# Routing one token tile ahead of the other, expert totals by 256 columns per bank, and one wave of last scatters

## The reference, cut to what matters

```
for l in range(DEPTH):                                   # 2 layers
    x = x + mixer(rms_norm(x)) @ w_out[l]
    h = rms_norm(x, norm_ffn_g[l])                       # 256 tokens
    g_idx = argmax(h @ wg + bg)                          # one group of 4
    top_val, top_idx = top_k(((h @ we + be) in group g_idx), 2)   # two of its 8 experts
    gates = softmax(groups)[g_idx] * softmax(top_val)
    y_e = (silu(h_e @ w_gate[e]) * (h_e @ w_up[e])) @ w_down[e]   # per expert e, its tokens h_e
    x = x + sum over the two experts of gates * y_e
```

## Time and profile before

| what | value |
|---|---|
| median of 3 runs | 1178.26 us (1177.89 to 1180.73) |
| profiled execution | 1179.48 us, span 1176.5 us |
| TensorE matmul busy | 884.6 us (75%) |
| VectorE busy | 469.5 us (40%) |
| ScalarE busy | 172.6 us (15%) |
| moved by DMA | 442.23 MB, mean 376 GB/s |
| TensorE clock granted, mean | 0.908 |

### The profile page before, as it was taken

How to read it: one execution, slowest core, us unless ns; L and a number is a source line. 1 busy time by engine, 2 the same in 40 slices (tenths; PEclk the granted TensorE clock), 3 DMA queues, 4 the chain that set the end, 5 groups by cost and what they waited for, 6 DMA issues and landing times.

```text
span 1176.5 us, 20445 instructions
## 1 busy us (share of the span) xinstructions
PE 884.6 (75%) x8557; PEld 531.7 (45%) x8557; DVE 469.5 (40%) x1263; ACT 172.6 (15%) x483; POOL 43.3 (4%) x98
## 2 busy tenths in 40 slices
PE   9999998675657565647799999977565666666777
PEld 6577574342424242424465675744233332323343
DVE  2967474331323232313239674743232322322222
ACT  2334211110000000100113442110000000000001
POOL 2001120000000000000000120000000000000000
PEclk9999998897979897988899999999889887879789
DMA  8946589999999999999996275999999999999996
GB/s 278 387 181 248 226 330 428 426 427 428 428 428 429 428 428 429 429 428 425 411 387 272 73 278 187 380 428 427 428 426 428 429 428 428 428 428 429 428 425 273
DMA packets 56141, 442.23 MB, mean 376 GB/s; under 512 B 9472, under 2 KB 12560, under 8 KB 30992
## 3 DMA queue, kind: packets, MB, share of 16 engines
q1 hardware_dynamic: 56080, 441.37, 90.8%
HBM read 440.30 MB, written 1.05 MB: 375 GB/s over the span
## 4 chain that ended last, share of the span: by engine, by line
PE 47%; DMA 44%; DVE 5%; issue 2%; SPq 1%; ACT 0%; DVEq 0%; POOL 0%; POOLq 0%
DMA ring<-in_expert_w_up 40%; PE psum L884 13%; PE psum L917 8%; PE psum L926 6%; PE psum L1001 5%; DMA work<-in_expert_w_down 4%; PE psum L898 3%; PE psum L763 3%; PE psum L857 2%; PE psum L1018 1%; PE psum L949 1%; DVE work L1522 1%; SPq L475 1%; PE psum L1128 1%; PE psum L744 1%
## 5 line engine op out<-in xcount | busy, mean ns | idle before, releaser
L884 PE MATMUL psum<-ring,work 128*32 128x256 f32 x3712 | 262.6, 444 | 111.3 <-DMA ring<-in_expert_w_up 111.3
L884 PEld LDWEIGHTS psum<-ring,work 128*32 128x32 f32 x3712 | 147.4, 127 | 224.3 <-issue 178.5
L898 PE MATMUL psum<-ring,work 128*32 128x256 f32 x1664 | 125.8, 454 | 126.6 <-DVE work L1528 126.2
L1520 DVE TENSOR_SCALAR work<-work 128x128 f32<-128x128 f32 x62 | 14.2, 229 | 344.0 <-ACT work L1206 344.0
L898 PEld LDWEIGHTS psum<-ring,work 128*32 128x32 f32 x1664 | 56.9, 128 | 191.5 <-DVE work L1528 148.8
L1533 DVE COPY work<-psum 32x256 f32<-32x256 f32 x124 | 52.6, 424 | 136.0 <-PE psum L898 134.9
L917 PE MATMUL psum<-ring,hT 128*128 128x512 f32 x224 | 98.5, 594 | 1.7 <-ACT work L1229 1.7
L1210 ACT ACTIVATE work<-psum 32x256 f32<-32x256 f32 x124 | 46.2, 373 | 267.1 <-PE psum L898 266.4
L763 PE MATMUL psum<-work,h 128*128 128x128 f32 x512 | 65.5, 290 | 14.2 <-issue 12.9
L763 PEld LDWEIGHTS psum<-work,h 128*128 128x128 f32 x512 | 64.3, 205 | 23.5 <-issue 23.5
L1206 ACT ACTIVATE work<-psum 128x128 f32<-128x128 f32 x62 | 17.2, 277 | 369.0 <-PE psum L884 339.7
(11 more groups left out here) (299 smaller groups left out, 780.6 us busy)
## 6 DMA issues: line engine op xcount, KB each, us to landing
ring<-in_expert_w_gate SPq DMA_DIRECT2D x64, 2048.0 KB, 18.4
ring<-in_expert_w_up SPq DMA_DIRECT2D x60, 2048.0 KB, 22.9
ring<-in_expert_w_down SPq DMA_DIRECT2D x52, 2048.0 KB, 22.7
ring<-in_w_in SPq DMA_DIRECT2D x10, 2048.0 KB, 18.4
work<-in_expert_w_down SPq DMA_DIRECT2D x6, 2048.0 KB, 14.8
ring<-in_w_out SPq DMA_DIRECT2D x4, 2048.0 KB, 8.6
ring<-in_w_in SPq DMA_DIRECT2D x8, 512.0 KB, 13.1
maps<-in_expert_w_down SPq DMA_DIRECT2D x2, 2048.0 KB, 8.7
```

The lines of the kernel that those rows point to most:

```text
L884: last = T.matmul(bank[GU_BANK[i % 2]][CAP * j:CAP * j + CAP, 0:2 * P], xg[:, k, CAP * i:CAP * i + CAP], gate_up[:, :, k, P * j:P * j + P] ...
L898: last = T.matmul(bank[5][CAP * q:CAP * q + CAP, 0:2 * P], actT[i % 2][:, CAP * j:CAP * j + CAP], down[j][:, 2 * P * q:2 * P * q + 2 * P], ...
```

## The change: what it does

Routing. Every step of the routing is written per tile, and the steps of tile 0 and tile 1 alternate in VectorE's queue. The first four of tile 0 stand inside `rsqrt` of tile 1. `log_ps`, `picks_ok`, `rank_ps` signal once per tile. Tile 0's half of `sel` is signalled by its own `sel_first`, and TensorE runs tile 0's half of the gather on it, then the totals per expert, then tile 1's half. The seed of tile 1 stands between the two ranks; two warming matmuls (L738, `keep_warm(2, 6)`) are gone. The two instructions that lead to ScalarE's exponentials stand later. `gate_values` is called ahead of `gathered`, as before right behind `sel`.

Totals. Bank `q` now holds columns 256 q to 256 q + 255 of both tiles, so seed and scatter are eight matmuls of 256 columns in place of four of 512; the transposes of the mixer's first tile use banks 5 and 6.

Tail. The last down weights come in three loads (1 MB, 0.5 MB, 0.5 MB). The fourth early scatter stands ahead of the second part. `last_scatter` is one wave of eight matmuls without waits, with one signal at its end, and a copy takes 2 x 256 columns from two banks. The output is stored in two transfers of 512 KB, each waiting for both engines' copies of its tile.

```diff
+        DOWN_PARTS = ((0, 1), (2,), (3,))
+        RANK_BANK, COUNT_BANK = (5, 7), 5
+        HT_BANK = (5, 6, 2, 3, 0, 1, 2, 3)
+        def sums(i, q):
+            return bank[q][:, i * 2 * P:i * 2 * P + 2 * P]
...
             # SyncE
-                e.wait_ge(log_ps.sem, log_ps.after(l, 1))
+                e.wait_ge(log_ps.sem, log_ps.after(l, TI))
-                e.wait_ge(seed_ps.sem, seed_ps.after(l, 4))
+                e.wait_ge(seed_ps.sem, seed_ps.after(l, TI))
-                for half in range(2):
-                    c = slice(half * SLOT // 2, half * SLOT // 2 + SLOT // 2)
-                    e.dma_start(slot(sd)[:, c], w_down[:, c]).then_inc(down_half[half].sem, 16)
+                for n, js in enumerate(DOWN_PARTS):
+                    c = slice(js[0] * SLOT // 4, (js[-1] + 1) * SLOT // 4)
+                    e.dma_start(slot(sd)[:, c], w_down[:, c]).then_inc(down_part[n].sem, 16)
             for i in range(TI):
-                for half, taken in enumerate((taken_dve, taken_act)):
-                    c = slice(half * 512, half * 512 + 512)
-                    e.wait_ge(taken.sem, taken.after(DEPTH - 1, i + 1))
-                    e.dma_start(out[0][i * P:i * P + P, c], x[:, i, c]).then_inc(out_done.sem, 16)
+                stream_ready(e, DEPTH, i)
+                e.dma_start(out[0][i * P:i * P + P], x[:, i, :]).then_inc(out_done.sem, 16)
...
             # TensorE, last_experts
+                early_scatter(0, 0)
                 e.wait_ge(up_half[0].sem, up_half[0].after(l, 16))
                 half_up(1, range(0, 4))
+                early_scatter(0, 1)
                 e.wait_ge(up_half[1].sem, up_half[1].after(l, 16))
                 half_up(1, range(4, KT)).then_inc(S.gu_ps.sem, 1)
+                early_scatter(1, 0)
...
-                half_down(0)
-                early_scatter(2)
-                half_down(1).then_inc(S.ye_ps.sem, 1)
-                early_scatter(3)
+                part_down(0)
+                early_scatter(1, 1)
+                part_down(1)
+                part_down(2).then_inc(S.ye_ps.sem, 1)
...
+                for t in range(TI):
+                    for q in range(QUARTERS):
+                        rows = slice(CAP * q, CAP * q + CAP)
+                        last = T.matmul(sums(t, q), spreadT[rows, t * P:t * P + P], ye_last[rows, :], start=False, stop=(t == TI - 1))
+                last.then_inc(tail_ps.sem, 1)
...
             # TensorE, behind router_logits(1)
+                seed(0)
                 e.wait_ge(picks_ok.sem, picks_ok.after(l, 1))
+                T.matmul(bank[RANK_BANK[0]][:, 0:NE], before[:, :], picks[:, 0, :], start=True, stop=True).then_inc(rank_ps.sem, 1)
+                seed(1)
+                e.wait_ge(picks_ok.sem, picks_ok.after(l, 2))
+                T.matmul(bank[RANK_BANK[1]][:, 0:NE], before[:, :], picks[:, 1, :], start=True, stop=False)
+                T.matmul(bank[RANK_BANK[1]][:, 0:NE], ones[:, :], picks[:, 0, :], start=False, stop=True).then_inc(rank_ps.sem, 1)
...
+                e.wait_ge(sel_first.sem, sel_first.after(l, 1))
+                gathered_tile(0)
+                T.matmul(bank[COUNT_BANK][:, 0:NE], ones[:, :], picks[:, 0, :], start=True, stop=False)
+                T.matmul(bank[COUNT_BANK][:, 0:NE], ones[:, :], picks[:, 1, :], start=False, stop=True).then_inc(count_ps.sem, 1)
+                e.wait_ge(h_ok.sem, h_ok.after(l, 2))
+                e.wait_ge(main.sel_ok.sem, main.sel_ok.after(l * GROUPS, 1))
+                gathered_tile(1)
...
             # VectorE
+                def scored(i): ...        # L1866 for one tile
+                def group_max(i): ...     # wait, settle, L1870
+                def group_found(i): ...   # wait, settle, L1874
+                def others_out(i): ...    # wait, L1877
+                def masked(i): ...        # wait, L1881
+                def expert_max(i): ...    # wait, settle, L1885
+                def expert_found(i): ...  # wait, settle, L1889
+                def chosen(i): ...        # wait, L1893, L1897
+                def picked(i): ...        # wait, L1896
+                def ranked(i): ...        # waits for rank_ps, L1901
+                def rank_of(i): ...       # wait, L1904
+                def coded(i): ...         # wait, L1907, L1908
+                def code_done(i): ...     # wait, L1910
+                def marked(i):
+                    e.wait_ge(c.sem, c.last())
+                    for n, dst in enumerate((sel, gtmp_first)):
+                        TS(dst[:, i, :], iota[:, :], codev[:, n, i:i + 1], rstd[:, i:i + 1], ALU.is_equal, ALU.mult).then_inc(c.step(), 1)
+                def selection(i, done):
+                    e.wait_ge(c.sem, c.last())
+                    TT(sel[:, i, :], sel[:, i, :], gtmp_first[:, i, :], ALU.add).then_inc(done.sem, 1)
...
+                rsqrt(rstd[:, 1:2], ssq[:, 1:2], D, [first_scored, first_max, lambda: group_found(0), lambda: others_out(0)])
+                masked(0)
+                scored(1)
+                expert_max(0)
+                group_max(1)
+                expert_found(0)
+                group_found(1)
+                chosen(0)
+                others_out(1)
+                picked(0)
+                masked(1)
+                expert_max(1)
+                ranked(0)
+                expert_found(1)
+                rank_of(0)
+                chosen(1)
+                coded(0)
+                picked(1)
+                code_done(0)
+                marked(0)
+                selection(0, sel_first)
+                ranked(1)
                 TS(nmg, mg[:, :, 0], -1.0, None, ALU.mult).then_inc(top_g.sem, 1)
                 TT(edif, mv[:, :, 1], mv[:, :, 0], ALU.subtract).then_inc(top_e.sem, 1)
+                rank_of(1)
+                coded(1)
+                code_done(1)
+                marked(1)
+                selection(1, main.sel_ok)
```

More of the change, by code:

```diff
@@ L1150, in _, with seed @@
[L1150 to L1153 removed]
+                def seed(i):
+                    for q in range(QUARTERS):
+                        last = T.matmul(sums(i, q), ident[:, :], x[:, i, q * 2 * P:q * 2 * P + 2 * P], start=(i == 0), stop=False)
+                    last.then_inc(seed_ps.sem, 1)
@@ new lines, in gathered_tile @@
+                def gathered_tile(i):
+                    for half in range(2):
+                        for k in range(4):
+                            last = T.matmul(bank[GU_BANK[half]][:, k * P:k * P + P], h[:, i, 4 * half + k, :], sel[:, i, :],
+                                            start=(i == 0 and k == 0), stop=(i == TI - 1 and k == 3))
+                        if i == TI - 1:
+                            last.then_inc(main.gath_ps.sem, 1)
+                e.wait_ge(h_ok.sem, h_ok.after(l, 1))
@@ L1904, in _ @@
[L1904 to L1910 removed]
+                logits = bank[4][:, 0:TI * 64].rearrange("p (i n) -> p i n", i=TI)
```

250 lines of the change are left out of this document (125 added, 125 removed).

## The result

The changed kernel takes 1181.78 us (median of 8, 1179.97 to 1182.98) against 1178.08 us (8 runs) for the kernel before in the same session: ratio 1.0028, 95% interval [1.0019, 1.0037]. The forecast was 1176.9 with a range up to 1180.0: wrong, in sign and in size. The profiled execution took 1181.7 us; its span is 1179.9 us, 3.4 us more than the 1176.5 of the kernel before.

What follows compares the result with a forecast made beforehand. Full DMA engines (427 GB/s) were taken to bound the experts' stretches, leaving their late start and serial tails to count. Tail -2.74, store -0.1, routing +1.5 made -1.35 us: 1178.26 to 1176.9, own range 1175.0 to 1178.8, wider 1173.3 to 1180.0.

Steps and rivals of the forecast that it cites:

- Routing, +1.5: Sums to first expert: per-tile steps delay `sel` by 1.4 us, the load's issue by 0.75 per layer, +1.5 for two.
- The rival of a shorter hand-over: Routing: interleaved steps hide latency, `sel` no later, gather's hidden half counts; total -4.1 us, 1174.1 us; chance 0.24.
- The settled steps' stall: Rival, routing: eight maxima and index steps each cost 0.35 us more, +2.8 per layer, 1182.5 us; chance 0.08.
- Tail, -2.74: Last down weights to copies of `x`: three terms shorten it by 1.37 us per layer, 2.74 for both.
- the scatter moved away: Tail, second term: the last scatter starts right after the copy, no longer behind an early scatter, -0.43 us per layer.
- one wave: Tail, third term: last scatter's eight matmuls without waits reach their copy in 1.1 instead of 1.53 us, -0.4 per layer.
- 256 columns "worth nothing": Scatters and seeds of 256 columns, inside the stretches where DMA engines are full: same columns in all, worth nothing there.
- Store, -0.1: Output store at the end: two transfers of 512 KB move the same bytes at about the same distance, -0.1 us.
- the first term of the tail: Last down weights: only 0.5 MB is used behind the last landing, -0.53 us per layer, bounds 0 and -0.53.
- the tail does not do what it says: Rival, tail: last landing's completion and serial matmuls leave about -0.5 us per layer; total +0.4, 1178.7 us; chance 0.13.

Runs made afterwards that it cites:

- e17: Changed kernel with the old routing and nine filler matmuls, cut into 36 of 128 columns, instead of four: 1176.58 us, ratio 0.9985 to the kernel before.
- e14: Changed kernel with nine filler matmuls, cut into 36 of 128 columns, instead of four: 1178.33 us, ratio 0.9999 to the kernel before.
- e12: Changed kernel with nine instead of four filler matmuls of 512 columns ahead of the last group's last unit: 1180.36 us, ratio 1.0011 to the kernel before.
- e2: Kernel before with the new routing alone, on its old totals, tail and store: 1180.40 us, ratio 1.0015.
- e7: Kernel before with each seed and scatter issued as two matmuls of 256 columns into the same bank: 1180.42 us, ratio 1.0018.
- e15: Kernel before with its four filler matmuls of 512 columns cut into 32 of 64, inside a wait for a load: 1179.74 us, ratio 1.0013.
- e1: Changed kernel with the old routing, four fillers kept: 1179.34 us, ratio 1.0010 to the kernel before.
- e8: Changed kernel with the old routing and nine instead of four filler matmuls of 512 columns: 1177.32 us, ratio 0.9993 to the kernel before.
- e16: Kernel before with nine instead of four filler matmuls of 512 columns ahead of the last group's last unit: 1177.54 us, ratio 0.9995.
- e9: Kernel before with 28 filler matmuls of 32 columns added ahead of the last group's last unit, where TensorE doesn't wait: 1196.08 us, ratio 1.0145.
- e10: e8 with selection and gather split by tile, picks and ranks kept together: 1177.58 us, ratio 0.9990 to the kernel before.
- e13: e10 with its nine fillers cut into 36 of 128 columns: 1174.61 us (6 runs), ratio 0.9968 to the kernel before.
- e11: e10 with 32 small filler matmuls added ahead of the last group's last unit: 1193.92 us, ratio 1.0124 to the kernel before.

## Why the prediction was wrong

Two steps failed. The tail's term took the last landing as what ends last; in the changed kernel that was TensorE, late by its clock and by the scatter put ahead of the landing. And the 256-column matmuls were put at nothing, while they brought a stall ahead of a load that the layer waited for.

The last four kernels of this table stand one edit apart and lead to the whole change; the first step holds several edits at once. The steps are differences of the ratios, times 1178.3:

```
before                                  1
end, totals, store; clock held,
  stall shifted (e17)                   0.9985    -1.8 us
+ new routing (e14)                     0.9999    +1.6
+ fillers uncut: stall at 759 (e12)     1.0011    +1.4
+ four fillers, not nine (the change)   1.0028    +2.0
```

The forecast was -1.35 us and the change measured +3.3. By the table the difference of 4.65 us is 2.0 for the clock, 1.4 for the stall, 1.0 for the end (-1.8 instead of -2.84) and 0.1 for the routing. Each step is uncertain by about 1.5 us (two intervals of some 1.1 us each), and the ratios come from four chips, so the sizes are rough and the step of 1.4 isn't clear of noise by itself. The signs are borne out by other pairs: the routing by e2, the stall by e7 and e15, the clock by e1 and e8.

- **Routing, +1.5: right.** `sel` came 11.54 us behind the sums (forecast 11.5), the first expert directly behind `xg`, +0.92 and +0.93 us at the issue (forecast +0.75): 16.90 after the sums, 16.7 forecast. Most of the miss is that L876 starts 0.83 us behind the start of the first `xg`, not 0.7. The rival of a shorter hand-over is dead: `sel` came later and not as early as before. The rule that a semaphore between chained VectorE instructions costs nothing (the Trainium skill, "VectorE: DVE Perf Modes", The DRAIN you can't avoid) doesn't hold for this chain of small ones, where the next one starts 0.20 us later with a wait and 0.08 without. The chain of the changed kernel also has more instructions, 53 records from the sums to `sel` instead of 44; no run separates their share of the 1.47 us from that of the waits. The settled steps' stall came once, 0.50 us in the first layer, as before.
- **Tail, -2.74: the step that failed.** It read "only 0.5 MB is used behind the last landing ... and the fourth early scatter is done by then", with bounds 0 and -0.53. It took the landing as what ends last. But in the first layer TensorE had waited only 0.44 us for the first down weights and 0.29 for the second, 0.73 in all, and the scatter moved ahead of them is 1.06 us of work (585.43 to 586.49). With the clock of before that alone makes TensorE some 0.3 us late, an estimate from these rows. On top, unit 2 ended 0.86 us later than the shift of the whole layer (0.59 and 0.92) explains, since it took 6.23 us instead of 5.26. Together that is about the 1.15 us by which the last down matmuls, at 586.49, are late against the same shift. They are those of both last parts (1.07, not 0.53), and from there it is 2.92 us to the first copy of `x` instead of 2.2. The first layer's end was 0.48 later, not 1.37 earlier. What stands behind the TensorE came as forecast: -0.35 for the scatter moved away (forecast -0.43), -0.32 for one wave (forecast -0.4). Only where the clock is held (e8, e12, e17) do the landings bound again. In e17 it is 1.0 us less from the last landing to the copy of `x`; the part of it that was forecast at -0.53 gives -0.32.
- **Clock: not in the sum.** In the second layer the granted clock from 1144 to 1150 was 1.00 before, and TensorE was busy all the time, by the rows still with what the stalls of 8.4 us at 1123 and 1129 had put off. In the changed kernel it waited 6.10 us for the load, and from 1151 to 1156 the granted clock was 0.65. In the first layer unit 2 was slow in both kernels. TensorE is late by what it loses there, and e12 gives 2.0 us back. That the loss is the clock's and not the fillers' own effect is borne out by e16: the same nine fillers give the kernel before, whose landings bound both ends, nothing that can be told.
- **256 columns "worth nothing": wrong**, though not by their columns. They add TensorE instructions to the program; a stall then falls ahead of the second layer's third load, and the one at 1129 is gone: +1.4 to +2.1 us (e14 to e12, e15, e7; e7 has the clock's part in it). The slot for that load is freed by TensorE, and the queue has run dry only some 10 us before: the rates fall again at 764 us. The prediction had taken every place inside the long stretch as covered by loads already issued.
- **Store, -0.1:** -0.57 from first copy to the end (5.65 to 5.08 us). That is about half of what the issues got shorter (0.93 instead of 2.04 us), which the prediction had taken as hidden.

With the first term of the tail at 0 the sum would have been about -0.3 (-1.66 - 0.1 + 1.5); the rival "the tail does not do what it says" (1178.7) had the right direction, and no rival held the stall or the clock. That the routing came out right is not luck: its marks came where the prediction put them.

Open: why the stalls lie where they do. Shown is that they move with instructions added elsewhere in the program: the kernel before has the one at 1129; with 5 more fillers a layer it is gone (e16); with 28 more a stall is at 757 (e9, e15); in e8, e10 and e12 it is there too, and 27 or 32 more take it away (e17, e13, e14, e11). Those near 540 and 1124 us come at the first instruction behind the loop over a layer's middle groups (the gather of the last group), in every trace. What happens in a stall, and by what rule it falls, no run shows. Whether it is the supply of instructions to TensorE wasn't tested; only their number was changed. That the stall kept the clock up in the kernel before is read from rows, not tested by itself.

## What to carry to other kernels

Before work is moved ahead of a landing, read how long the engine waits for it, and for those just before it: the move is free only up to that sum (0.73 us in the first layer, for 1.06 us of work), and the wait itself depends on the engine's clock. Splitting a serial chain by tiles paid here where the consumer can start on the half (selection and gather: the load 0.5 us earlier per layer), not in the chain ahead of it (load 0.92 us later). When adding instructions costs time and no row shows why, compare where the "issue" stalls lie in both traces, and shift them with fillers inside a wait.

## What the runs showed of the hardware

TensorE has waits of 1.5 to 5.3 us for which the profile shows no semaphore. Those near 188, 540, 771 and 1124 us are there in all profiled kernels (later by what e9 and e11 lose); another comes and goes with some 30 matmuls more or less elsewhere in the program, and its price runs from nothing that can be told (at 1129: the kernel before against e16) to about 1.5 us (at 757: e15). Behind the stall at 757 the granted clock fell to 0.50 for about 3 us in five of eleven traces. A stall may help as well: by the rows of the kernel before, it kept TensorE busy until the load was there and so kept its clock. That wasn't tested by itself.

After a wait of 6.10 us for a load the granted clock was 0.65 over 5 us, and 64 matmuls took 5.36 instead of 3.66 us. With nine fillers of 512 columns in that wait (e12), or 36 of 128 (e14), they took 3.66.
